# Weights split in whole units with two slots instead of half units with four, in a two-block fp32 transformer on one core

## The reference, cut to what matters

```python
def first_block(x, p, ...):
    a = rmsnorm(h, attn_norm[i])
    proj = a @ w_in[i]
    oa = hgrn2_mixer(aq, af, ai, ag, lbs[i], hgrn_onorm[i])
    ob = fox_mixer(bq, bk, bv, bf, fox_bf[i], fox_qnorm[i], fox_knorm[i])
    oc = moba_mixer(cq, ck, cv, moba_qnorm[i], moba_knorm[i], slopes)
    h = h + jnp.concatenate([oa, ob, oc], axis=-1) @ w_out[i]
    c = rmsnorm(h, ffn_norm[i])
    h = h + conv_ffn(c, w_gate[i], w_up[i], conv_w[i], conv_b[i], w_down[i])
    e = rmsnorm(h, ple_norm[i])
    h = h + jax.nn.sigmoid(e @ w_ple_gate[i]) * (p[i] @ w_ple_proj[i])

def second_block(x, c, w_mod, b_mod, ...):
    mod = silu(c) @ w_mod + b_mod            # six vectors: shifts, scales, gates
    h = rmsnorm_2(x, attn_norm_g) * (1.0 + sc1) + sh1
    # sliding-window attention and latent attention on h @ w_in, then w_out
    h = rmsnorm_2(x, mlp_norm_g) * (1.0 + sc2) + sh2
    u = relu(h @ w_ff1)
    x = x + g2 * ((u * u) @ w_ff2)
```

## Time and profile before

| | before |
|---|---|
| median of 3 runs | 2540.63 us |
| lowest, highest | 2538.52, 2541.36 us |
| span of the profiled execution | 2547.7 us |
| other time of the profiled execution | none is shown |
| mean granted TensorE clock | 0.980 |
| TensorE busy | 2419.6 us, 95% |
| VectorE busy | 1946.2 us, 76% |
| ScalarE busy | 1092.2 us, 43% |
| HBM | 202 GB/s over the span |

### The profile page before, as it was taken

One profiled execution on the slowest core, in us unless ns is written; L12 is line 12 of the kernel. 1 busy time (PEld: TensorE's weight loads), 2 busy tenths in 40 slices (PEclk: granted clock), 3 DMA queues, 4 the chain that ended last, 5 costly groups with the idle time before them and its releaser, 6 DMA issues.

```text
span 2547.7 us, 37180 instructions
## 1 busy us (share of the span) xinstructions
PE 2419.6 (95%) x13460; PEld 2057.7 (81%) x13460; DVE 1946.2 (76%) x3035; ACT 1092.2 (43%) x1472; POOL 115.0 (5%) x221
## 2 busy tenths in 40 slices
PE   6979999989999999999988989899899999999997
PEld 5868787878888888888877867778788888888886
DVE  4688677779998989898976756676777777777775
ACT  4334444444434344444345444644444344334432
POOL 0100000000000000000000010000000000000000
PEclk8989999999999999999999989999999999999999
DMA  5754466357887878778864544334355555545552
GB/s 198 270 186 149 154 225 215 139 196 261 286 289 266 284 260 281 273 277 284 277 214 153 207 161 159 116 102 162 134 187 193 183 183 187 193 169 193 185 183 82
DMA packets 86666, 516.76 MB, mean 203 GB/s; under 512 B 9861, under 2 KB 10389, under 8 KB 37360
## 3 DMA queue, kind: packets, MB, share of 16 engines
q1 hardware_dynamic: 57168, 407.93, 44.8%
q0 software_dynamic: 29200, 106.31, 12.4%
q10 hardware_dynamic: 144, 0.26, 0.0%
HBM read 509.22 MB, written 5.24 MB: 202 GB/s over the span
## 4 chain that ended last, share of the span: by engine, by line
PE 86%; DVE 8%; ACT 3%; DMA 2%; issue 2%; SPq 0%; DVEq 0%; POOLq 0%; ACTq 0%
PE ps L464 47%; PE ps L465 24%; PE ps L462 5%; PE ps L461 2%; PE ps L482 2%; DMA modraw<-in_wmod 2%; PE ps L532 1%; DVE wl L1147 1%; DVE yn L1246 1%; ACT wh L776 1%; PE ps L541 1%; DVE modraw L1200 1%; PE ps L580 1%; DVE xs L1233 1%; PE ps L550 0%
## 5 line engine op out<-in xcount | busy, mean ns | idle before, releaser
L464 PE MATMUL ps<-xs,wh 128*128 128x512 f32 x4003 | 1462.6, 406 | 41.5 <-DVE xs L1233 17.3
L776 ACT ACTIVATE wh<-raw 128x1024 fp32r<-128x1024 f32 x768 | 809.9, 1058 | 1077.6 <-PE ps L462 810.1
L1147 DVE TENSOR_TENSOR wl<-raw,wh 128x1024 fp32r<-128x1024 f32 x768 | 937.3, 1222 | 317.7 <-ACT wh L776 301.6
L465 PE MATMUL ps<-xs,wl 128*128 128x256 f32 x4003 | 1131.5, 283 | 0.0
L464 PEld LDWEIGHTS ps<-xs,wh 128*128 128x128 f32 x4003 | 761.0, 190 | 242.4 <-issue 42.4
L465 PEld LDWEIGHTS ps<-xs,wl 128*128 128x128 f32 x4003 | 766.0, 191 | 11.3
L464 PE MATMUL ps<-hs,wh 128*128 128x512 f32 x1504 | 543.5, 400 | 5.7 <-DVE hs L1506 3.3
L465 PE MATMUL ps<-hs,wl 128*128 128x256 f32 x1504 | 423.1, 281 | 0.0
L464 PEld LDWEIGHTS ps<-hs,wh 128*128 128x128 f32 x1504 | 284.2, 189 | 65.4 <-DVE hs L1506 3.6
L465 PEld LDWEIGHTS ps<-hs,wl 128*128 128x128 f32 x1504 | 285.5, 190 | 10.0
L1200 DVE CUSTOM_DVE_ANT_0 modraw<-modraw,cb 128x1024 f32<-128x1024 f32 x192 | 233.4, 1218 | 24.8 <-DMA modraw<-in_wmod 24.6
(11 more groups left out here) (210 smaller groups left out, 1493.8 us busy)
## 6 DMA issues: line engine op xcount, KB each, us to landing
raw<-in_w SPq DMA_DIRECT2D x384, 1024.0 KB, 4.9
modraw<-in_wmod POOLq DMA_DIRECT2D x192, 512.0 KB, 4.3
rel_rows<-rrow POOLq DMA_DIRECT2D x4, 768.0 KB, 3.9
x<-in_x SPq DMA_DIRECT2D x4, 512.0 KB, 6.1
tbias<-rel_rows POOLq DMA_DIRECT2D x16, 128.0 KB, 2.8
out_dram<-mix SPq DMA_DIRECT2D x4, 512.0 KB, 2.6
hmask<-in_hmask SPq DMA_DIRECT2D x1, 512.0 KB, 17.3
mix<-in_p ACTq DMA_DIRECT2D x1, 256.0 KB, 4.2
```

The lines of the kernel that those rows point to most:

```text
L464: nc.tensor.matmul(out[:, :], hi[:, w], pair, start=s, stop=e)
L465: m = nc.tensor.matmul(out[:, 0:T], lo[:, w], src[:, k, 0, :], start=False, stop=e, skip_group_check=e)
L776: nc.scalar.activation(wh[:, h % HS, :], raw[:, u % RAW, (h % 2) * 1024:(h % 2 + 1) * 1024], ACT.Copy).then_inc(s_round, 1)
L1147: nc.vector.tensor_tensor(wl[:, h % HS, :], raw[:, (h // 2) % RAW, (h % 2) * 1024:(h % 2 + 1) * 1024], wh[:, h % HS, :].bitcast(F32), ALU. ...
```

## The change

Rounding and subtracting are done for a whole unit of 128x2048 at once. `wh` and `wl` keep their size, but are now two slots of a unit instead of four of a half. `rnd(h)` and `sub(h)` do nothing in odd halves; in the even half h they work on unit h/2 + 1, so the look-ahead is one unit. `rnd` then waits until both halves of the unit two before are used. TensorE waits for `s_split` once a unit. `s_split` and `s_round` count units. Ahead of the first norm one unit is split where three halves were.

```diff
-HS = 4
-LOOK = 3
+WS = 2
...
+    def unit(self, value):
+
+        step = self.per.get("h", 0) // 2
         return value + self.i * step if step else value
...
-        wh = at("wh", [P, HS, 1024], 32, F32R)
-        wl = at("wl", [P, HS, 1024], 48, F32R)
+        wh = at("wh", [P, WS, 2048], 32, F32R)
+        wl = at("wl", [P, WS, 2048], 48, F32R)
...
-                    sp.wait_ge(s_split, i * (2 * RAW) + 2 * r + 2)
+                    sp.wait_ge(s_split, i * RAW + r + 1)
...
-                    pe.wait_ge(s_split, c.val("h", hh + 1))
-                    hi, lo = wh[:, hh % HS, :], wl[:, hh % HS, :]
+                    if half == 0:
+                        pe.wait_ge(s_split, c.unit(hh // 2 + 1))
+                    hi, lo = (v[:, hh // 2 % WS, half * 1024:(half + 1) * 1024] for v in (wh, wl))
...
-                if h < 2 * UNITS:
-                    u = h // 2
-                    if h % 2 == 0:
-
-                        v = 16 * (u // RAW + 1)
-                        act.wait_ge(s_raw[u % RAW], v + c.i * (c.per["h"] * 16 // (2 * RAW)) if c.per else v)
-                    if h >= HS:
-
-                        act.wait_ge(s_used, c.val("h", h - HS + 1))
-                    nc.scalar.activation(wh[:, h % HS, :], raw[:, u % RAW, (h % 2) * 1024:(h % 2 + 1) * 1024],
-                                         ACT.Copy).then_inc(s_round, 1)
+                u = h // 2 + 1
+                if h % 2 == 0 and u < UNITS:
+                    v = 16 * (u // RAW + 1)
+                    act.wait_ge(s_raw[u % RAW], v + c.i * (c.per["h"] * 16 // (2 * RAW)) if c.per else v)
+                    if u >= WS:
+
+                        act.wait_ge(s_used, c.val("h", 2 * (u - WS) + 2))
+                    nc.scalar.activation(wh[:, u % WS, :], raw[:, u % RAW, :], ACT.Copy).then_inc(s_round, 1)
...
-                    rnd(c.n["h"] + LOOK)
+                    rnd(c.n["h"])
...
-            for h in range(LOOK):
-                rnd(h)
+            rnd(-2)
...
-                if h < 2 * UNITS:
-                    dve.wait_ge(s_round, c.val("h", h + 1))
-                    nc.vector.tensor_tensor(wl[:, h % HS, :], raw[:, (h // 2) % RAW, (h % 2) * 1024:(h % 2 + 1) * 1024],
-                                            wh[:, h % HS, :].bitcast(F32), ALU.subtract).then_inc(s_split, 1)
+                u = h // 2 + 1
+                if h % 2 == 0 and u < UNITS:
+                    dve.wait_ge(s_round, c.unit(u + 1))
+                    nc.vector.tensor_tensor(wl[:, u % WS, :], raw[:, u % RAW, :], wh[:, u % WS, :].bitcast(F32),
+                                            ALU.subtract).then_inc(s_split, 1)
...
-                sub(c.n["h"] + LOOK)
+                sub(c.n["h"])
...
-            for h in range(LOOK):
-                sub(h)
+            sub(-2)
```

More of the change, by code:

```diff
@@ L95, in val @@
         step = self.per.get(name, 0)
+        return value + self.i * step if step else value
+    def unit(self, value):
+        step = self.per.get("h", 0) // 2
         return value + self.i * step if step else value
@@ L390, in _ @@
                 u = RAW * (rounds + 1) + r
-                sp.wait_ge(s_split, 2 * (u - RAW) + 2)
+                sp.wait_ge(s_split, u - RAW + 1)
                 sp.dma_start(raw[:, r, :], a["w"][u, :, :]).then_inc(s_raw[r], 16)
```

## The result

The changed kernel takes 2581.38 us, the median of four runs (2579.87 to 2587.22), against 2539.72 us for the kernel before. The ratio is 1.0168, with a 95% interval of 1.0154 to 1.0182: 42 us slower. The forecast was 2572 us in a range of 2552 to 2600, slower.

A forecast was written before the change was run, and what follows sets the result against it. TensorE, 95% busy, was taken to bound the kernel, so the change acts only through waits. Terms 12.4 + 0.2 + 4.4 + 17.3 - 2.8 = 31.5 us gave 2572 us, 1.2% slower, range 2552 to 2600.

The forecast's parts named there:

- four norms and start: TensorE waits 3.1 us for the wide subtraction behind each of four norms, 12.4 us; 0.2 us at the first norm.
- nine places in even halves: Small results TensorE wants one half later stand behind a wide operation; 0 to 1.9 us each, 1.5 taken, 14 us.
- steady sliding-window units: Some eight units have subtraction, 2.3 us of job and next transposes in line; about 0.25 us each, 2 us.
- start of stage B: A 3.78 us wait for a rounding goes, but take and subtraction wait for whole units; chain ends 1.3 us later.
- PLE projection and q up-projection: Odd halves copy without a rounding ahead; saves 1.3 us in the PLE projection and 1.5 in the q up-projection.
- stage A: Loop closes through the w_mod buffers, so its 14.1 us period per two units stays; nothing, bounds -4 and +10 us.
- clock: Lower clock after each of four new norm waits costs 0 to 1.7 us; 1.1 taken each, 4.4 us in all.
- Durations: The 128x2048 subtraction on VectorE takes 2.29 us and the rounding on ScalarE 1.91 us, by lines through narrower sizes.
- Steady units: FFN gate units fill VectorE's queue for 5.45 of 5.65 us, with 1.2 us of slack; no cost.
- first rival: Slack in steady FFN units is too thin; 0.2 us on each of 260 units, 52 us, 2624 us; chance 0.07.
- second rival: VectorE's saving counts in A, B and the norms; 4.5 us and B's 3.78 us wait gained, 2532 us; chance 0.05.

The follow-up runs named there:

- second profile of before: The kernel before, profiled once more with no edit; 2538.04 us, span 2536.4 us.
- added operation: Changed kernel with one unused 128x512 VectorE operation behind each gate unit's conv chain, ahead of the wide subtraction; 2612.99 us, ratio 1.0283.
- late order: Kernel before with subtractions moved behind the bias copy and sliding-window job steps, and the rounding behind the latent squares; 2524.16 us, ratio 0.9928.
- `LOOK = 2`: Kernel before, narrow operations and slots filled by halves, but splitting two halves ahead instead of three; 2555.07 us, ratio 1.0049.

## Why the prediction was right, and where its sizes were off

The direction, the places and the mechanism were right, and the time was 9 us low. That it was only 9 is in part luck: the clock cost 17 us more than forecast, and the waits at the loops' borders, which I had not looked at, gave back 6.6. By terms, against the second profile of before (waits over 0.25 us on TensorE's timeline):

| term | forecast | measured |
|---|---|---|
| four norms and start | 12.6 | 11.7 at the norms |
| nine places in even halves | 14 | 12.3, in seven of them |
| steady sliding-window units | 2 | 1.6 |
| start of stage B | 1.3 | 1.3 |
| PLE projection and q up-projection | -2.8 | -2.6 |
| stage A | 0 | 1.7 |
| places not named | none | 2.8 |
| squares at the norms | none | -0.4 |
| borders of the FFN and second MLP loops | none | -6.6 |
| waits in all | 27.1 | 22.1 (0.3 not placed) |
| clock | 4.4 | 21.1 |

- **Durations and the norms: right.** 3.1 us each was forecast, 3.00, 2.92, 2.87 and 2.87 came. (I had given TensorE's last matmul 0.35 us; the earlier trace rows have 0.28.)
- **Places in even halves: right as a sum.** (Nine at 1.5 us are 13.5; I had written 14.) HGRN's rstd 1.2, MOBA 2.1, last h 1.4, bias copy 2.0, latent squares 0.9, first sliding-window job 2.7, rotary 2.0. Both head norms' tails were covered. Not named were the second V copy (0.85), the forget gate's scan (0.44) and three early squares behind a wide rounding in the PLE gate (0.5 each).
- **Steady units: right.** A gate unit's queue was put at 5.45 us and VectorE is busy 5.48 of 5.65 us; TensorE never waits. The added operation confirms the room of 0.2 us. So the first rival was close. It was priced in steady units alone; with the added operation the loop's borders cost 9.5 us more, and the clock 4.
- **Stage A: the reasoning failed, the size is not shown.** I had said that its period of 14.1 us for two units would stay and that I was wrong if it changed. In the changed kernel two units there take 10.2 to 13.1 us. But in the second profile of before they take 10.2 to 12.8, and with the late order, the same program up to there, 13.5 to 14.5. So the 14.1 of the earlier trace rows comes and goes with the execution and is no fixed period of the kernel. The 1.7 us of the table are smaller than this difference between executions.
- **Clock: the step that failed.** I counted it for the four norms alone, 1.1 us each, from one stretch of six microseconds, and put it at nothing everywhere else without a reason. Nothing in my own rows limited it to norms: the chain places have waits as long. At the norms it was about right: the 6 us behind the four waits have a mean granted clock of 0.52, 0.72, 0.76 and 1.00. The share missing from 6 us is 2.9, 1.7, 1.4 and 0 us, 6.0 in all where 4.4 were forecast. Over the whole span, before has 98 us at the 1.2 GHz level, in 18 stretches, and the changed kernel 144 us in 25. The second input stage went from 34 to 49 us, the first half of the first output projection from 3 to 10, B with C from 3 to 9, FFN from 6 to 15, its last downs with the PLE projection from 4 to 11, the PLE gate from 3 to 9 and the second output projection from 0 to 8. The start of stage B and the second half of the first output projection have 8 us less. In C one such stretch, at 319 to 322 us, has no wait over 0.25 us in the 38 us ahead of it. Half of the 47 us is 23 us, and TensorE's busy time grew by 21.1. The Trainium skill, "TensorE: Matmul & The Clock Gate", section "Terms", prices time at the reduced clock in the same way, at that time times the share of pulses withheld; the traces agree within 3 us.
- **Loop borders: missed, in the change's favour.** The first profile of before has them at 796.90, 934.96 and 1073.73, and I did not ask what they are. In the FFN loop they stand (0.9 to 3.4 us) in the seven kernels where TensorE waits for each half, wide subtraction or not, and in none of the five where it waits once a unit and VectorE is not loaded further. That points to the number of waits against a loop's register on TensorE; no run changed that alone, so it stays open.
- **The second rival** (VectorE's saving counts) failed: VectorE is busy 42 us less, and none of the six stretches above got shorter. By the rule of the Trainium skill quoted ahead ("Perfetto Trace Analysis", "Optimizing Scalar/DVE Operations"), its second half is what happened: narrow operations let the first half be used sooner, and going back to them at the same unit window (2550.72) returned 34 of the 42 us.

## What to carry to other kernels

A producer that is ahead on average is not ahead everywhere. Look for the places where a small result that the bottleneck awaits stands in the same queue behind bulk work that has slack, and put the small work first: in the kernel before this alone gave 0.7%, while no kernel with wide operations was faster than its narrow counterpart. And when waits of a microsecond or more appear on TensorE, price the clock with them at once: here 22 us of new waiting came with 21 us of slower matmuls, and the late order in the kernel before took away 11.9 us of waiting and 5.9 us of busy time.

## What the runs showed of the hardware that I had not expected

- A wait far shorter than the 3.3 us of the earlier trace rows can be followed by a stretch at the lower clock. With `LOOK = 2` the waits of 2.16 to 2.91 us at the FFN loop's borders are each followed by one; in the second profile of before 1.95 us at 1062.54 is, and 1.45 and 1.69 us at the two borders ahead of it are not. The length of the wait does not decide alone. The 3.32 us wait of the earlier trace rows stands in the second profile of before too, at 1293.50, and the 6 us behind it are at full clock; so are those behind the 2.87 us wait at the last norm of the changed kernel:

```profile
1293.50:1299.50 6.00, 6.00 (x34) 5.22 (x35) 2.71 (x6) 1.12 (x2) 0.00 (x0) 1.00 0.70 239
```

```profile
1839.84:1845.84 6.00, 6.00 (x34) 5.20 (x35) 3.55 (x5) 0.42 (x1) 0.00 (x0) 1.00 0.74 244
```

So the stretch from which I took the price of the clock came out the other way in another execution, and a price per wait taken from one such stretch can be wrong by the whole of it.
- Stage A of the same program ended at 145.78 and at 138.0 us in two executions, and at 149.0 us in the kernel before with the late order, which is the same program up to there. VectorE's waits for the w_mod transfers in it are 19.1, 8.2 and 22.6 us in the same order. A single profile of this kernel can thus be off by 10 us without any wait that a change made. Why the transfers land later in one execution than in another was not tested.
